# A two-block transformer kernel on one core: order of the slab remainders, the decay scans and the value products around a gated recurrence

## The reference, cut to what matters

```python
q, f, i, g = split(h @ hg_w_in)                     # 6 heads of 128, 512 tokens
q = silu(q) * 128**-0.5
fg = lb + (1 - lb) * sigmoid(f);  k = 1 - fg;  logf = log(fg);  v = i
b = cumsum(logf)                                    # inside a chunk
o[t] = sum over s <= t of (q[t] * exp(b[t] - b[s]) * k[s]) @ v[s]      # per head
o = rms_norm(o, g_out) * silu(g)
m = softmax(rms_norm(qm) @ rms_norm(mem_k).T * 64**-0.5) @ mem_v       # 4 heads, 256 memories
x = x + concat(o, m) @ w_out;   x = x + conv_ffn(rms_norm(x))
```

## Time and profile before

| what | value |
|---|---|
| three timed executions | 1852.2, 1852.47, 1852.59 us (median 1852.47) |
| the profiled execution's own time | 1851.83 us |
| its span, first to last instruction | 1850.0 us (1.83 us lie around it) |
| mean granted PE clock | 0.964 of full |
| busy: PE, PEld, DVE, ACT, POOL | 95%, 77%, 49%, 41%, 38% |
| memory keys to last `hq` | about 495 to 582 us |
| memory attention | 582 to 650 us |
| recurrence, six heads | 650 to 788 us |

### The profile page before, as it was taken

How to read it: one execution, slowest core, us unless ns; L and a number is a source line. 1 busy time by engine, 2 the same in 40 slices (tenths; PEclk the granted TensorE clock), 3 DMA queues, 4 the chain that set the end, 5 groups by cost and what they waited for, 6 DMA issues and landing times.

```text
span 1850.0 us, 24845 instructions
## 1 busy us (share of the span) xinstructions
PE 1750.2 (95%) x8605; PEld 1427.9 (77%) x8605; DVE 898.4 (49%) x1689; ACT 762.8 (41%) x1174; POOL 699.3 (38%) x362
## 2 busy tenths in 40 slices
PE   5999899999998998989999999999887999999999
PEld 4778566888886788878888888877755788888887
DVE  4587566458326266645555531143455355555200
ACT  4332455337343434244444533324333354444322
POOL 2334211444533455334444444433200344444444
PEclk9999999999998988799999999999897899999999
DMA  5233211333322201022323233332200232323333
GB/s 180 81 114 92 68 47 35 103 101 105 114 77 72 80 26 33 12 69 91 96 97 98 95 102 103 102 97 59 68 1 1 62 98 91 101 92 101 93 112 114
DMA packets 43421, 151.75 MB, mean 82 GB/s; under 512 B 4944, under 2 KB 5072, under 8 KB 43344
## 3 DMA queue, kind: packets, MB, share of 16 engines
q1 hardware_dynamic: 41184, 145.16, 25.3%
q10 hardware_dynamic: 2160, 5.53, 0.9%
HBM read 148.58 MB, written 2.10 MB: 81 GB/s over the span
## 4 chain that ended last, share of the span: by engine, by line
issue 49%; PE 25%; POOL 22%; DVE 2%; ACT 1%; DMA 1%; POOLq 0%; ACTq 0%; DVEq 0%
POOL WL L556 21%; PE DB L635 4%; PE DB L636 4%; PE DB L637 4%; PE SC L937 2%; PE SC L741 2%; PE DB L766 1%; PE DB L685 1%; PE DB L686 1%; PE DB L687 1%; PE OB L755 1%; PE TB L635 1%; PE DB L755 1%; DMA CONST<-in_consts_dram 1%; PE TB L636 0%
## 5 line engine op out<-in xcount | busy, mean ns | idle before, releaser
L556 POOL TENSOR_TENSOR WL<-RAW,WH 128x1024 fp32r<-128x1024 f32 x268 | 643.1, 2400 | 1141.9 <-ACT WH L1143 1141.8
L1143 ACT ACTIVATE WH<-RAW 128x1024 fp32r<-128x1024 f32 x268 | 284.0, 1060 | 736.3 <-PE DB L637 302.3
L635 PE MATMUL DB<-XH,WH 128*128 128x512 f32 x584 | 244.0, 418 | 5.4 <-DVE XL L1610 3.2
L1011 PE MATMUL DB<-XH,WH 128*128 128x512 f32 x640 | 249.0, 389 | 0.0
L1012 PE MATMUL DB<-XL,WH 128*128 128x512 f32 x640 | 249.0, 389 | 0.0
L1013 PE MATMUL DB<-XH,WL 128*128 128x512 f32 x640 | 249.0, 389 | 0.0
L636 PE MATMUL DB<-XL,WH 128*128 128x512 f32 x584 | 232.5, 398 | 0.0
L637 PE MATMUL DB<-XH,WL 128*128 128x512 f32 x584 | 232.0, 397 | 0.0
L635 PEld LDWEIGHTS DB<-XH,WH 128*128 128x128 f32 x584 | 112.6, 193 | 41.7 <-issue 14.9
L1013 PEld LDWEIGHTS DB<-XH,WL 128*128 128x128 f32 x640 | 120.1, 188 | 25.1
L1012 PEld LDWEIGHTS DB<-XL,WH 128*128 128x128 f32 x640 | 120.1, 188 | 24.9
(11 more groups left out here) (447 smaller groups left out, 3001.3 us busy)
## 6 DMA issues: line engine op xcount, KB each, us to landing
RAW<-in_stream_dram SPq DMA_DIRECT2D x268, 512.0 KB, 3.5
TP<-in_toep_dram ACTq DMA_DIRECT2D x4, 512.0 KB, 3.6
out_dram<-X SPq DMA_DIRECT2D x8, 256.0 KB, 4.2
X<-in_xt_dram SPq DMA_DIRECT2D x4, 256.0 KB, 5.1
X<-in_xt_dram ACTq DMA_DIRECT2D x4, 256.0 KB, 5.4
MRAW<-in_memt_dram ACTq DMA_DIRECT2D x2, 512.0 KB, 5.3
CONST<-in_consts_dram ACTq DMA_DIRECT2D x1, 448.0 KB, 9.9
MSKI<-in_masks_dram ACTq DMA_DIRECT2D x1, 288.0 KB, 2.9
```

Source lines behind the costliest of these rows:

```text
L556: nc.gpsimd.tensor_tensor(WL[:, s, :], RAW[:, j, :], WH[:, s, :].bitcast(F32), ALU.subtract).then_inc(lo_done, 1)
L635: mm(o, WH[:, s, c], hi(k), start=(k == 0), stop=False)
L1011: mm(o, WH[:, s, c], xh(k), start=(k == 0), stop=False)
L1143: A(WH[:, n % SPLIT, :], RAW[:, n % RING, :], ACT.Copy).then_inc(hi_done, 1)
```

## The change

Six edits, none of which adds or removes arithmetic or a transfer:

1. POOL: the slab remainder of the next head's gate is made after a head's last difference instead of after its second; that of the first head's gate stays after the second difference of head 0.
2. PE: the value products wait for the copies of levels 7, 8 and 9 separately; the diagonal product of each block comes first, and only the last two products wait for level 9.
3. Memory keys: all four copies are made first, into four halves of two buffers, and spread into four halves of two banks; DVE waits for two spreads at a time.
4. DVE: the six scans are made as soon as the logarithms are there; `root_scaled` of `hq0`, `hq1` and `hq2` stand before scans 0, 2 and 4, those of `hq3` to `hq5` after `decays_ready`.
5. PE, memory attention: the value pieces run (0, 2, 2, 2, 2, 2, 2, 2, 1, 1, 0) by step instead of two a step from step 2.
6. ACT: `next_slab` runs one step earlier, and `hv0` is emptied in step 4.

```diff
@@ gpsimd
-                    if l == 1:
-                        low((s0 + h + (h > 0)) % RING, s0 + h + (h > 0))
-                    if h == 0 and l == 4:
-                        low((s0 + 1) % RING, s0 + 1)
+                    if h == 0 and l == 1:
+                        low(s0 % RING, s0)
+                    if l == 7:
+                        low((s0 + h + 1) % RING, s0 + h + 1)
@@ tensor
-            def attention(seg, banks_read, beside=None, pieces=1):
+            def attention(seg, banks_read, beside=None, pieces=lambda k: 2 * (k >= 2)):
-                    for _ in range(pieces if beside is not None and k >= 2 else 0):
+                    for _ in range(pieces(k) if beside is not None else 0):
                         next(beside, None)
@@ head_spread
-                if q >= 2 and name[:2] != "ho":
+                if q >= 4 and name[:2] != "ho":
+                if group == "mk":
+                    c = slice(MEM * (q % 2), MEM * (q % 2) + MEM)
+                    bank_, src = (SC[1], OB)[q // 2][:, c], RH[q // 2][:, c]
@@
-            attention(segments["m0"], [], itertools.chain(*(token_tiles(f"hv{k}", xh, xl, 384) for k in range(2))), 2)
+            attention(segments["m0"], [], itertools.chain(*(token_tiles(f"hv{k}", xh, xl, 384) for k in range(2))),
+                      lambda k: (0, 2, 2, 2, 2, 2, 2, 2, 1, 1, 0)[k])
@@
-                pe.wait_ge(lv_cp, n)
+                pe.wait_ge(lv_cp, n - 2)
                 for i in range(NT):
-                    for j in range(i + 1):
+                    for j in range(i, -1, -1):
+                        if (j, i) == (0, 1):
+                            pe.wait_ge(lv_cp, n - 1)
+                        if (j, i) == (1, 3):
+                            pe.wait_ge(lv_cp, n)
@@ scalar, next_slab
-                if s["g"] % 2 and k >= 2:
-                    while split_next[0] <= JOBS["hv0"].slabs[0] + k + (k == 7):
+                if s["g"] % 2 and k >= 1:
+                    while split_next[0] <= JOBS["hv0"].slabs[0] + k + 1:
-                if s["g"] % 2 and k == 5:
-                    job_ready("hv0")
+                if s["g"] % 2 and k == 4:
+                    act.wait_ge(slab_used, JOBS["hv0"].done)
                     values(0)
@@ vector
-                dve.wait_ge(hs_rb, q + 1)
+                dve.wait_ge(hs_rb, q - q % 2 + 2 if name[:2] == "mk" else q + 1)
+                if name[:2] == "mk":
+                    return (SC[1], OB)[q // 2][:, MEM * (q % 2):MEM * (q % 2) + MEM]
@@
-            head_copy("mk", 0)
-            head_copy("mk", 1)
+            for a in range(4):
+                head_copy("mk", a, RH[a // 2][:, MEM * (a % 2):MEM * (a % 2) + MEM])
             root_scaled("hf0")
             for a in range(4):
-                if 1 <= a < 3:
-                    head_copy("mk", a + 1)
@@
             for k in range(HG):
-                root_scaled(f"hq{k}")
+                if k % 2 == 0:
+                    root_scaled(f"hq{k // 2}")
                 dve.wait_ge(hf_ln, k + 1)
...
             V.drain().then_inc(decays_ready, 1)
+            for k in range(3, HG):
+                root_scaled(f"hq{k}")
```

More of the change, by code:

```diff
@@ L854, in _ @@
             pe.wait_ge(*emptied("va"))
-            attention(segments["ab"], [emptied("gb3")], itertools.chain(*(feature_tiles(f"za{k}", xh, xl) for k in range(KD))), 2)
+            attention(segments["ab"], [emptied("gb3")], itertools.chain(*(feature_tiles(f"za{k}", xh, xl) for k in range(KD))))
             assert JOBS["zb0"].bank() != 3
@@ L961, in _ @@
                 for i in range(NT):
-                    for j in range(i + 1):
+                    for j in range(i, -1, -1):
[3 more added lines that the diff above has]
+                            pe.wait_ge(lv_cp, n)
                         a = PT[:, h % 2, P * i:P * i + P] if j == i else AX[:, slot[j, i], :]
-                        last = mm(OB[:, P * i:P * i + P], HV[:, j, P * h:P * h + P], a, start=(j == 0), stop=(j == i))
+                        last = mm(OB[:, P * i:P * i + P], HV[:, j, P * h:P * h + P], a, start=(j == i), stop=(j == 0))
                 last.then_inc(ho_mm, 1)
```

## The result

The changed kernel took 1837.70 us, median of four runs (1832.53 to 1838.68), against 1852.34 beside it: a ratio of 0.9917, 95% interval 0.9898 to 0.9936, so 15 us or 0.8% faster. I had predicted 1839.4. The profiled execution is the fastest of the four: 1832.53 us, of which 1830.7 are span, at a mean granted clock of 0.970; the other three had 0.966. Before it was 1850.0 at 0.964.

A forecast was written before the change was run, and what follows sets the result against it. PE's waits, and the low granted clock behind the longest, were taken as the bound. Keys 2.1 + scans 5.4 + 0.9 + clock 3.5 - 0.7 - 0.3 + products 2.1 = 13.0 us off 1851.83: 1838.8, median 1839.4, range 1833 to 1846.

The forecast's parts named there:

- Keys: Memory keys: all copies made first, so PE's two waits at the spreads go; 2.1 us gained, lower end 1.6.
- Scans: Before the attention: moved scans let the first maximum follow hq5, shortening PE's wait for the second scores; 5.4 us gained.
- 0.9 for the step behind: Memory attention: PE's 0.86 us wait before step 2's scores goes too; 0.9 us gained.
- Clock in the attention: Attention: the 7.90 us at clock 0.50 behind the long wait runs at 1.00; 3.5 us gained, lower end 1.7.
- Wait for `hv0` moves, nothing: Attention: the 2.5 us wait for emptying hv0 only moves from step 6 to step 5; nothing gained.
- Late remainder: At hq2: scan 1 would delay a POOL slab remainder that PE waits for; 0.7 us lost, ends 0 and 0.8.
- Collision in head 4: Head 4: POOL's moved remainder meets DVE's three root copies, making them later; 0.3 us lost, ends 0 and 1.4.
- Value products: Recurrence: 0.52 us waits before value products go in all heads, paying behind heads 0, 1, 2 and 4; 2.1 us.
- Open clock: Everything behind 517 us: granted clock may shift either way; no net change taken, plus or minus 6 us.
- The slower rival: Recurrence: heads 1, 2, 3 and 5 all run at 0.70 like head 4; about 22 us more, 1861; chance 0.03.
- the rivals: Smaller gains: recurrence gives nothing, 9.8 us (0.13); slabs replace attention wait, 6.7 (0.07); change misses what was late, 4.2 (0.08).

The follow-up runs named there:

- keys_alone: Kernel before with only the memory-key copies and their spreads and scalings changed; median 1845.8 us, ratio 0.9958–1.0.
- scans_and_slabs: Kernel before with the scans moved ahead and the value slabs and pieces a step earlier; median 1850.5 us, ratio 0.9951–0.9999.
- scans_alone: Kernel before with only the scans moved ahead, value slabs and pieces staying a step later; median 1843.8 us, ratio 0.9945–0.9985.
- three_more: Changed kernel with DVE's gate behind level 2's weighing, ACT's norm square root behind head 3, scan 1 behind hq1's scaling; median 1826.1 us.
- roots_early: three_more with the reciprocal and three DVE root copies moved from head 4 into DVE's idle time in head 3; median 1821.4 us.
- heads_alone: Kernel before with only the slab remainder behind the last difference and the separate value-product waits; median 1845.9 us, ratio 0.9949–0.9975.
- changed_filled: Changed kernel with one needless 128x384 matmul before level 2 of heads 1, 2 and 3; median 1833.0 us, ratio 0.9892–0.9922.
- products_alone: Kernel before with only the separate value-product waits, POOL's remainder still before the level 2 difference; median 1873.4 us, ratio 1.0102–1.0132.
- without_heads: Changed kernel with the moved slab remainder and the separate value-product waits undone; median 1834.8 us, ratio 0.9913–0.9972.

## Why the prediction was right

- **Keys, 2.1 us.** Measured 2.6 in keys_alone as in the changed kernel. The copies ran as worked out.
- **Scans, 5.4 us, and 0.9 for the step behind.** The first maximum stands behind `hq5`, the waits fell from 7.2 to 0.9, and scans_and_slabs against scans_alone shows that the 0.9 belongs to slabs and pieces (0.8).
- **Clock in the attention, 3.5 us.** Attention fell by 10.9 us, of which 6.3 are waits; the clock there went from 0.89 to 1.00. The term was about 1 us small: before, the wait for `hv0` had a stretch at 0.50 behind it (3.4 us), and in the changed kernel the same wait of 2.5 us had none. In three_more and roots_early it has one again, and the attention takes 52.2 and 52.4 us; so this microsecond is luck. "Wait for `hv0` moves, nothing" was right for the wait only.
- **Late remainder, 0.7.** PE's wait at `hq2` is 1.15 against 0.41, and the stage 0.65 us longer. POOL does wait for a DVE scan that came first. The Trainium skill says so (SBUF — State Buffer, section "SBUF: two separate sides": whichever of the two starts first holds the shared ports for its whole instruction): the trace agrees, 553.55 + 1.22 = 554.77 and from there 2.18 us to the remainder's end, near the 2.4 that one takes alone.
- **Collision in head 4, 0.3 with ends 0 and 1.4.** Mis-sized in kind: the copies took 2.25 us in the changed kernel and PE, at 1.2 GHz, did not wait at all; it waited 0.74 in heads_alone, 1.95 in changed_filled and 3.20 in three_more. The upper end was taken from a stretch at the low clock, where PE is slow enough to hide it.
- **Value products, 4 x 0.52 = 2.1.** 19.15 to 18.26 in heads at 1.00: 0.89 a head, 3.6 in all. Of this 0.12 a head is the remainder's, which takes 19.15 to 19.03 by itself. I took the recorded idle time and not the distance from start to start. That POOL's edit is needed for it is shown by products_alone. It is shown stage by stage and at equal clock, not by the totals (without_heads). Behind heads 3 and 5 it is given back as said: the wait behind head 5 went from 1.95 to 3.6.
- **Open clock, plus or minus 6.** Over the recurrence the clock was 0.85 before and after, so the zero held there, by balance and not because nothing moved. By those means the clock's share of the 4.7 us is about 1 (an estimate: 0.15 x 139.8 against 0.15 x 135.1), which leaves about the 3.6 of the products. At an equal recorded clock, 0.966, before took 1848.1 and 1848.2 (two executions) and the changed kernel 1837.6 to 1838.7: 9.4 to 10.6, where the terms without the clock make 13.0 - 3.5 = 9.5. The rest of the 14.6 is clock, and it is not steady: executions of one kernel lie up to 22.9 us apart.
- **The slower rival, 0.03.** Its mechanism is real: products_alone is what it describes, at 1873 and not 1861. The whole change escaped it since POOL's edit kept the wait before level 2 at 0.9. I had weighed it by "no more idle time than before"; products_alone has little more idle time either, but in longer pieces.

The totals of the rivals are 0.2 to 0.3 us low in the prediction: 1852.47 less 9.8, 6.7 and 4.2 is 1842.7, 1845.8 and 1848.3. That changes none of its chances.

That the forecast came within 2 us of the median is in part luck. The second set of the changed kernel has 1833.9, 5.5 us from it, and the sum's own figure, 1838.8 for a profiled execution, stands against 1832.5. By stages the sum had 2.1 for the keys, a loss of 0.7 at the scans, 9.8 for the attention and 1.8 for the recurrence; the profiles show 2.6, 0.7, 10.9 and 4.7, and 1.6 us more where nothing was changed (ahead of the keys and behind head 5). So the order and the mechanism of the terms held, and the sizes were on the whole too small.

What stays open is why the slower executions of one kernel lose their clock, and why kernels with the same waits in the recurrence ran it at 0.78, 0.85 and 0.89 (151.5 to 151.7, 139.8 and 134.0 us). A profile shows one execution, and none is of a slow execution of the changed kernel.

## What to carry to other kernels

Merging two short waits of PE into one longer can cost many times the wait, through the granted clock (21 us here), and filling it can bring that back; so look at the idle pieces that an edit leaves, and how long each is, and not at their sum alone. The length alone does not decide either: the same waits were followed by different clocks in different kernels. To size an edit where the clock varies, compare the same stage at the same granted clock, start to start, and compare totals only between executions of equal mean clock. A collision that a slow engine hides becomes its bound once the engine is fast: after each gain look at what the covered terms cost at full speed.

## What was unexpected of the hardware

- Two needless matmuls in each of three waits of 1.8 us made a kernel 25.7 us faster (1873.4 to 1847.7). The Trainium skill (TensorE: Matmul & The Clock Gate, part 1) has the throttled state as the default and activity as what releases it; the trace agrees: the three heads ran at 0.64, 0.69 and 0.73 with PE idle in these waits, and at 1.00 with PE at work.
- The scatter of a kernel's executions depends on the kernel: 29 executions of before lie within 5.7 us, twelve of scans_and_slabs over 21.7, in step with their mean clock (0.972 to 0.959). With its keys edited alone the times form two groups 15 us apart.
- Three DVE copies of 128x512 took 1.10 us alone, 1.52 before, with two POOL differences beside them, 2.25 (the changed kernel) and 4.16 us (three_more) with a POOL remainder and differences beside them.
